# Last stage of a decoder block: row additions and splits on DVE, norm weights folded into the gate weights, finish of tiles after all additions

## Chip, cores and metric

The kernel runs on one core of a Trainium2 chip. The metric is the device time of one execution in microseconds; lower is better. Times of the kernel before are the median of three executions. One further execution was profiled, and every row below is from it.

## What is computed

One layer of a decoder over 512 tokens of 1024 float32 values. After attention and a mixture of experts it ends in a gated embedding and a norm; this end is the stage that the change rewrites:

```
h = h + moe_ffn(rmsnorm(h, g_ffn), ...)            # 8 expert rows per token, weighted, summed
h = h + (p @ w_ple) * sigmoid(rmsnorm(h, g_ple) @ w_ple_gate)
return rmsnorm(h, g_final)

def rmsnorm(x, g):
    r = rsqrt(mean(x * x, axis=-1) + 1e-6)
    return (x * r) * g
```

## The kernel before

The 512 tokens are four tiles (`NT`) of 128 partitions, the 1024 columns eight chunks (`KD`) of 128. Work is written by hand per engine; each engine runs its instructions in order and waits on semaphores (`E[...]` in the expert steps, `T[...]` in the last stage). The expert steps (`experts_*`) write each weighted expert row to `expert_rows` in HBM, 4096 rows of 1024 values (16 MB). The last stage (`tail_*`) does for each tile t:

- SP loads the tile's eight rows per token: tile 0 in four transfers of 1 MB ("quarters"), tiles 1 to 3 in two transfers of 2 MB each, n = 2 to 7, into four buffers of `ring`. Transfer n from 4 on waits for `took` to reach n - 3.
- `add_rows(t)`: the eight rows are added up and onto `h`. For tile 0 DVE does all (L1841, L1843). For tiles 1 to 3 DVE folds the first half (L1851, L1853) and adds it onto `h` (L1855), POOL folds the second half (L1732, L1734), and DVE adds that onto `h` (L1858, waits for `added`). Each addition onto `h` raises `took`.
- `turn_tile(t)` on PE transposes the tile, eight 128x128 blocks (L1759), after `took`.
- ACT takes them from PSUM, times `g_ple`, rounded to the format of the fast float32 product (`halves`, eight of 128x128, L1799); DVE computes what the rounding left off (`rests`, eight of 128x128, L1865).
- `gate_half(t, i)`: with each operand as a rounded part and a rest, PE needs three products per chunk, so 24 matmuls for each of the two column halves (L1774). `turn_tile(t + 1)` stands between the two halves.
- `squares`: ACT sums the squares of `h` (L1804), POOL makes the root (`root`, L1723 and L1725), ACT takes the sigmoid (L1812), `gated` on DVE multiplies by the embedding and adds onto `h` (L1873, L1875), then squares and a root again, and `finish` scales (L1880). SP stores the tile.

The gate weights `w_ple_gate` are split in the same way: ACT rounds (`wg_hi`, L1583), POOL computes the rest (`wg_lo`, L1720). DVE's order in `tail_vector` is written out; in the middle of it stand `gated(0)`, `rests(2)`, `finish(0)`, `add_rows(3)`, `gated(1)`, `rests(3)`, `finish(1)`.

Of the kernel before, what the change touches and what calls it, by code (L numbers as in the profile page):

```python
# [108 lines left out]
def build(nc, a, dbg=None):  # L109
# [8 lines left out]
    with ctx:  # L118
# [1434 lines left out]
        def experts_scalar(act):
# [9 lines left out]

            rows_in(0)
            for s in range(NS):
# [220 lines left out]
        def tail_scalar(act):
# [4 lines left out]
            act.wait_ge(s_gpk, 16)  # L1791

            def halves(t):
                if t >= 2:
                    act.wait_ge(T["mm"], 8 + 2 * (t - 1))
                for half in range(2):
                    act.wait_ge(T["turned"], 1 + 2 * t + half + 1)
                    for k in range(4 * half, 4 * half + 4):
                        last = nc.scalar.activation(x3[t % 2][:, 0, k, :], bank[BX3[t % 2][half]][:, (k % 4) * P:(k % 4 + 1) * P], ACT.Copy, scale=gpk[:, k:k + 1])  # L1799
                    last.then_inc(T["x_hi"], 1)  # L1800

            def squares(t, name, o):
                act.drain()
                nc.scalar.activation(junk, h[:, t, :], ACT.Square, scale=D ** -0.5, accum_out=part[:, o + t:o + t + 1]).then_inc(T[name], 1)  # L1804

            def sigmoids(t):
                act.wait_ge(T["rr"], t + 1)
                for i in range(2):
                    act.wait_ge(T["mm"], 8 + 2 * t + i + 1)
                    if t:  # L1810
                        act.wait_ge(T["gated"], 2 * (t - 1) + i + 1)
                    nc.scalar.activation(sigt[:, i * 512:(i + 1) * 512], bank[BG[t % 2][i]][:, :], ACT.Sigmoid, scale=part[:, 4 + t:5 + t]).then_inc(T["sig"], 1)  # L1812

            def last_squares(t):
                act.wait_ge(T["h3"], t + 1)
                squares(t, "ss2", 8)
# [141 lines left out]
```

## Time and profile before

| | us |
|---|---|
| median of 3 executions (lowest, highest) | 1277.23 (1275.13, 1278.48) |
| the profiled execution, its own time | 1278.9 |
| its span, first to last instruction | 1277.1 |
| busy in the span: PE, DVE, ACT, POOL | 1135.0, 472.5, 276.7, 320.2 |
| last expert matmul to the end of the span | 1156.7 to 1277.1 |

Times in rows are microseconds from the start of the span. A row of the timeline merges instructions that follow each other with the same line and operation (x gives how many) and names in brackets how long the engine had been idle before and what ended that. PE's clock has two levels, 1.2 and 2.4 GHz; "PEclk" is the granted share of the higher one.

### The profile page before, as it was taken

What the parts mean: (1) busy time and instruction counts of PE and PEld (TensorE: products, weight loads), DVE (VectorE), ACT (ScalarE), POOL (GpSimd) and SP (SyncE); (2) the same over time, 40 slices, a digit from 0 to 9 for tenths busy, and PEclk for the clock granted to TensorE, in tenths of its full rate; (3) what the DMA queues carried; (4) which work ended last, traced back from release to release, by engine and by line L of the source; (5) the groups of instructions that cost most, each with busy time, mean ns of one, the idle gap of its engine ahead of it and who ended that gap; (6) DMA issues with size and microseconds to landing.
All of it is one profiled execution on the core that took longest, in us unless ns stands there. A gap on an engine that the chain in (4) does not pass through costs nothing.

```text
span 1277.1 us, 19026 instructions
## 1 busy us (share of the span) xinstructions
PE 1135.0 (89%) x7561; PEld 663.3 (52%) x7562; DVE 472.5 (37%) x1050; ACT 276.7 (22%) x641; POOL 320.2 (25%) x218
## 2 busy tenths in 40 slices
PE   5999999999989899779999988998898999896476
PEld 4888786776767797434543333333333333332365
DVE  5245654564465634652222111211112211114475
ACT  3123333333345200101111111111111111114122
POOL 5522533333233210001111111111111111117360
PEclk9999999999989899779999988988999999998687
DMA  9821312222115124407999999999999999997611
GB/s 285 222 55 34 84 47 70 50 59 58 34 34 173 52 83 184 195 17 298 412 357 388 422 422 423 417 416 409 417 407 406 420 411 404 413 361 297 253 52 50
DMA packets 118424, 306.20 MB, mean 240 GB/s; under 512 B 21792, under 2 KB 80320, under 8 KB 92352
## 3 DMA queue, kind: packets, MB, share of 16 engines
q1 hardware_dynamic: 106096, 270.88, 55.6%
q0 software_dynamic: 12240, 34.09, 6.7%
q8 instruction: 61, 1.00, 0.3%
q14 instruction: 27, 0.22, 0.0%
HBM read 289.21 MB, written 26.21 MB: 247 GB/s over the span
## 4 chain that ended last, share of the span: by engine, by line
PE 25%; DMA 17%; issue 5%; POOL 3%; POOLq 2%; SPq 1%; DVE 0%; ACT 0%; ACTq 0%
DMA sb_gate_up<-in_w_up 17%; PE bank L1408 15%; PE bank L1432 7%; PE bank L1398 2%; POOL sb_w_gate_lo L1720 2%; POOLq L1733 1%; POOL sb_rows L1734 1%; SPq L963 1%; SPq L1443 0%; POOLq L1724 0%; PE bank L1415 0%; SPq L967 0%; POOL sb_small L1725 0%; PE bank L920 0%; DVE sb_xgT L1529 0%
## 5 line engine op out<-in xcount | busy, mean ns | idle before, releaser
L1408 PE MATMUL bank<-sb_gate_up,sb_xgT 128*32 128x512 f32 (+2 forms) x2144 | 312.6, 625 | 42.4 <-DMA sb_gate_up<-in_w_up 41.5
L1408 PEld LDWEIGHTS bank<-sb_gate_up,sb_xgT 128*32 128x32 f32 (+2 forms) x2144 | 98.3, 121 | 225.4 <-issue 221.4
L457 PE MATMUL bank<-sb_x_hl,sb_w_hl 128*128 128x512 f32 x768 | 200.4, 405 | 0.0
L1474 POOL DMA_INDIRECT expert_rows<-sb_rows_out,sb_work x42 | 42.2, 1004 | 474.4 <-DVE sb_rows_out L1535 474.4
L457 PEld LDWEIGHTS bank<-sb_x_hl,sb_w_hl 128*128 128x128 f32 x768 | 138.0, 189 | 43.5 <-issue 16.0
L1432 PE MATMUL bank<-sb_down,sb_work 128*32 128x512 f32 (+2 forms) x1072 | 153.3, 595 | 1.6 <-ACT sb_work L1573 0.6
L241 POOL TENSOR_TENSOR sb_w_hl<-sb_r,sb_w_hl 128x1024 fp32r<-128x1024 f32 x54 | 131.9, 2446 | 64.0 <-ACT sb_w_hl L1149 52.1
L1543 DVE TENSOR_TENSOR sb_work<-sb_work,bank 128x256 f32<-128x256 f32 x42 | 17.8, 423 | 333.2 <-ACT sb_work L1567 333.2
L235 POOL CAST sb_w_hl<-sb_r 128x1024 fp32r<-128x1024 f32 x35 | 37.6, 1075 | 205.6 <-PE bank L457 158.2
L1567 ACT ACTIVATE sb_work<-bank 128x256 f32<-128x256 f32 x42 | 16.2, 386 | 330.6 <-PE bank L1408 330.6
L1432 PEld LDWEIGHTS bank<-sb_down,sb_work 128*32 128x32 f32 (+2 forms) x1072 | 47.6, 116 | 73.3 <-issue 69.2
L770 ACT ACTIVATE sb_h<-sb_h,sb_small 128x128 f32<-128x128 f32 (+3 forms) x96 | 53.3, 556 | 133.3 <-DVE sb_small L665 133.2
L665 DVE CUSTOM_DVE_ANT_0 sb_h<-bank,sb_bias 128x128 f32<-128x128 f32 (+3 forms) x96 | 43.3, 488 | 103.7 <-PE bank L490 102.7
L1535 DVE TENSOR_SCALAR sb_rows_out<-bank,sb_work 128x512 f32<-128x512 f32 x42 | 31.5, 751 | 126.2 <-PE bank L1432 126.2
L956 POOL DMA_INDIRECT sb_xg<-xn_rows,sb_work x42 | 43.0, 1025 | 101.5 <-PE bank L1398 45.0
L1562 ACT ACTIVATE sb_rows_out<-bank,sb_work 128x512 f32<-128x512 f32 x42 | 28.9, 687 | 154.6 <-PE bank L1432 154.6
L1398 PEld LDWEIGHTS bank<-sb_cst,sb_xg 128*128 128x128 f32 x336 | 41.0, 192 | 34.5 <-issue 34.5
L1034 PE MATMUL bank<-sb_w_hl,sb_x_hl 128*128 128x256 f32 x384 | 48.6, 290 | 5.6 <-DVE sb_x_hl L1198 5.6
L1034 PEld LDWEIGHTS bank<-sb_w_hl,sb_x_hl 128*128 128x128 f32 x384 | 48.1, 199 | 6.0 <-issue 6.0
L1398 PE MATMUL bank<-sb_cst,sb_xg 128*128 128x128 f32 x336 | 47.8, 285 | 1.6 <-PEq L969 1.6
L780 ACT COPY sb_work<-bank 128x128 f32<-128x128 f32 (+4 forms) x104 | 40.3, 437 | 37.7 <-PE bank L503 32.5
L1022 PE MATMUL bank<-sb_x_hl,sb_w_hl 128*128 128x512 f32 x192 | 45.4, 399 | 2.9 <-PEq L372 2.9
(254 smaller groups left out, 1326.9 us busy)
## 6 DMA issues: line engine op xcount, KB each, us to landing
sb_gate_up<-in_w_gate SPq DMA_DIRECT2D x64, 1024.0 KB, 18.3
sb_gate_up<-in_w_up SPq DMA_DIRECT2D x64, 1024.0 KB, 24.3
sb_down<-in_w_down SPq DMA_DIRECT2D x64, 1024.0 KB, 18.2
sb_r<-in_w_in SPq DMA_DIRECT2D x34, 512.0 KB, 3.9
sb_rows<-expert_rows SPq DMA_DIRECT2D x6, 2048.0 KB, 9.3
sb_r<-in_w_out SPq DMA_DIRECT2D x8, 512.0 KB, 3.8
sb_rows<-expert_rows SPq DMA_DIRECT2D x4, 1024.0 KB, 7.8
sb_h<-in_x SPq DMA_DIRECT2D x4, 512.0 KB, 8.1
```

The costliest lines, as they stand in the source:

```text
L241: nc.gpsimd.tensor_tensor(w6_hl[:, slot, 1], raw_at[buf], w6_hl[:, slot, 0].bitcast(F32), ALU.subtract).then_inc(s_split, 1)
L457: last = nc.tensor.matmul(out[:, :], w6_hl[:, slot_at[n], zw, k, :], x_hl[:, zx, k, :], start=k + i == 0, stop=k == KD - 1 and i == 2)
L665: nc.vector.tensor_tensor_reduce(out=sc[:, i % 3, hh, 0:n_of(u)], in0=bank[BS[hh]][:, 0:n_of(u)], in1=bias[:, u["pair"] % 2, hh, S - n_of( ...
L770: nc.scalar.activation(sc[:, i % 3, hh, 0:n_of(u)], sc[:, i % 3, hh, 0:n_of(u)], ACT.Exp, scale=-1.0, bias=minus_max[:, i % 4, hh:hh + 1], ...
L780: nc.scalar.copy(pT[rows, i % 2, hh, 0:n], bank[BT[hh]][rows, 0:n]).then_inc(F["copied"], 1)
L956: nc.gpsimd.indirect_dma_start(out=xg[s % 2], out_offset=None, in_=xn2_d, in_offset=bass.IndirectOffsetOnAxis(ap=idx[:, s:s + 1], axis=0), ...
L1022: last = nc.tensor.matmul(bank[2 * (m % 4) + i][:, :], w6_hl[:, SLOT_OF[m], zw, k, :], x_hl[:, zx, k, :], start=k % 4 + j == 0, stop=k % 4 ...
L1034: last = nc.tensor.matmul(bank[t][:, (q % 2) * 256:(q % 2 + 1) * 256], x_hl[:, zx, k, t * P:(t + 1) * P], w6_hl[:, lo:lo + 2, zw, k, :], s ...
L1398: last = nc.tensor.transpose(bank[BX[half]][:, (k % 4) * P:(k % 4 + 1) * P], rows[:, k, :], ident)
L1408: last = nc.tensor.matmul(bank[BH][rows, :], xgT[:, k, rows], gate_up[slot_of[r]][:, :, k, :], start=k == 0, stop=k == KD - 1)
L1432: last = nc.tensor.matmul(bank[BO[i]][rows, :], hT[:, c, rows], Wd[slot_of[r]][:, c, i * 512:(i + 1) * 512], start=c == 0, stop=c == 1)
L1474: nc.gpsimd.indirect_dma_start(out=rows_d, out_offset=bass.IndirectOffsetOnAxis(ap=dst[:, s:s + 1], axis=0), in_=osb[s % 2], in_offset=Non ...
```

## The change

It moves no work before the last two expert steps. In the last stage:

1. POOL keeps only the roots. The folding of the second half of tiles 1 to 3 goes to DVE, in the same form as the first. The rests of the gate weights go to DVE too (`rest_of_gate`): two ahead of the last `rows_out` of the expert steps, six ahead of `add_rows(0)`.
2. `g_ple` is folded into the gate weights: `wg_hi` is the rounded product of weight and `g_ple`, `wg_lo` the rest of that product. The transposed tile is then only copied and subtracted, two instructions of 128x512 each on ACT and DVE in place of eight of 128x128. ACT rounds weight chunks 6 and 7 ahead of the copies of the turned `p` and of its last `rows_out`; the other six stay behind.
3. DVE's order is: additions and rests of all four tiles, then `gated(0)`, `gated(1)`, `finish(0)`, `gated(2)`, `finish(1)`, `finish(2)`, `gated(3)`, `finish(3)`. There are two buffers for the sigmoid.
4. Squares are summed by column halves, POOL adds the two sums (one more instruction per root); the second squares start on the first half. The sigmoid's table is loaded after the embeddings.
5. `turn_tile(t + 1)` stands after the first four chunks of `gate_part(t, 1)`.
6. SP issues `gfin` after the gate weights instead of before them.

```diff
@@ experts_sync @@
-            sp.dma_start(gfin, a["g_final"].partition_broadcast(P)).then_inc(s_gp, 16)
             w_gate_ple = chunks(a["w_ple_gate"][0])
...
                 sp.dma_start(wg_in[g][:, :, :], w_gate_ple[:, k:k + n]).then_inc(s_wg[g], 16)
+            sp.dma_start(gfin, a["g_final"].partition_broadcast(P)).then_inc(s_gp, 16)
@@ before rows_out(NS - 1) of experts_vector (n = 0, 1) and at the start of tail_vector (n = 2 to 7) @@
+        def rest_of_gate(n):
+            k = WG_ORDER[n]
+            nc.vector.wait_ge(T["w_hi"], n + 1)
+            nc.vector.scalar_tensor_tensor(out=wg_lo[k], in0=wg_raw[k], scalar=gpk[:, k:k + 1], in1=wg_hi[k].bitcast(F32),
+                                           op0=ALU.mult, op1=ALU.subtract).then_inc(T["w_lo"], 1)
@@ experts_scalar @@
+            for k in (6, 7):
+                round_gate(k)
             act.wait_ge(T["turned"], 1)
             for c in range(2):
                 nc.scalar.copy(pTt[:, c, :], bank[BX[c]][:, :]).then_inc(T["turned_sb"], 1)
             rows_out(NS - 1)
...
-                nc.scalar.copy(wg_hi[k], wg_raw[k]).then_inc(T["w_hi"], 1)
+            for k in range(6):
+                round_gate(k)
@@ tail_gpsimd @@
-                nc.gpsimd.tensor_tensor(wg_lo[k], wg_raw[k], wg_hi[k].bitcast(F32), ALU.subtract).then_inc(T["w_lo"], 1)
...
+                nc.gpsimd.tensor_tensor(part[:, o + t:o + t + 1], half_sums[:, o + 2 * t:o + 2 * t + 1], half_sums[:, o + 2 * t + 1:o + 2 * t + 2], ALU.add)
+                pool.drain()
...
-                nc.gpsimd.tensor_tensor(r[:, 0:2, :], r[:, 0:2, :], r[:, 2:4, :], ALU.add)
-                pool.drain()
-                nc.gpsimd.tensor_tensor(r[:, 0, :], r[:, 0, :], r[:, 1, :], ALU.add).then_inc(T["added"], 1)
@@ tail_tensor @@
             turn_tile(0)
             for t in range(NT):
-                gate_half(t, 0)
+                pe.wait_ge(T["x_lo"], 2 * t + 2)
+                gate_part(t, 0, range(KD))
+                gate_part(t, 1, range(4))
                 if t + 1 < NT:
                     turn_tile(t + 1)
-                gate_half(t, 1)
+                gate_part(t, 1, range(4, KD))
@@ tail_scalar @@
-                        last = nc.scalar.activation(x3[t % 2][:, 0, k, :], bank[BX3[t % 2][half]][:, (k % 4) * P:(k % 4 + 1) * P], ACT.Copy, scale=gpk[:, k:k + 1])
+                    nc.scalar.copy(x3[t % 2][:, 0, 4 * half:4 * half + 4, :], psv(BX3[t % 2][half], 4, P)).then_inc(T["x_hi"], 1)
...
             sigmoids(2)
-            last_squares(2)
-            sigmoids(3)
-            last_squares(3)
+            squares(0, "ss2", 8)
+            squares(1, "ss2", 8)
+            sigmoids(3, (0,))
+            squares(2, "ss2", 8)
+            sigmoids(3, (1,))
+            squares(3, "ss2", 8)
@@ tail_vector @@
-                dve.wait_ge(T["added"], t)
-                nc.vector.tensor_tensor(h[:, t, :], h[:, t, :], ring[(n + 1) % 4][:, 0, :], ALU.add).then_inc(T["took"], 1)
+                for n in (2 * t, 2 * t + 1):
+                    r = ring[n % 4]
+                    dve.wait_ge(s_rows[n % 4], 16 if n < 6 else 32)
+                    nc.vector.tensor_tensor(r[:, 0:2, :], r[:, 0:2, :], r[:, 2:4, :], ALU.add)
+                    dve.drain()
+                    nc.vector.tensor_tensor(r[:, 0, :], r[:, 0, :], r[:, 1, :], ALU.add)
+                    dve.drain()
+                    nc.vector.tensor_tensor(h[:, t, :], h[:, t, :], r[:, 0, :], ALU.add).then_inc(T["took"], 1)
+                    dve.drain()
...
+                    nc.vector.tensor_tensor(x3[t % 2][:, 1, ks, :], psv(BX3[t % 2][half], 4, P), x3[t % 2][:, 0, ks, :].bitcast(F32), ALU.subtract).then_inc(T["x_lo"], 1)
...
+            for t in range(NT):
+                add_rows(t)
+                rests(t)
             gated(0)
+            gated(1)
             finish(0)
+            gated(2)
             finish(1)
             finish(2)
             gated(3)
             finish(3)
```

The order of instructions on DVE before, from the last addition of tile 2 to the start of tile 3's additions (`sb_rows_*` are the buffers of `ring`, t_added is POOL's folding, t_rr2 the second root):

```order
L1858 TENSOR_TENSOR sb_h<-sb_h,sb_rows_5515 128x1024 [waits t_added]
L1873 TENSOR_TENSOR sb_emb<-sb_emb,sb_sig_ple 128x512 [waits t_sig]
L1875 TENSOR_TENSOR sb_h<-sb_h,sb_emb 128x512
L1873 TENSOR_TENSOR sb_emb<-sb_emb,sb_sig_ple 128x512 [waits t_sig]
L1875 TENSOR_TENSOR sb_h<-sb_h,sb_emb 128x512
L1865 SCALAR_TENSOR_TENSOR sb_x_0_5490<-bank,sb_g_ple,sb_x_0_5490 128x128 [waits t_x_hi]
L1865 SCALAR_TENSOR_TENSOR sb_x_0_5490<-bank,sb_g_ple,sb_x_0_5490 128x128 x3
L1865 SCALAR_TENSOR_TENSOR sb_x_0_5490<-bank,sb_g_ple,sb_x_0_5490 128x128 [waits t_x_hi]
L1865 SCALAR_TENSOR_TENSOR sb_x_0_5490<-bank,sb_g_ple,sb_x_0_5490 128x128 x3
L1880 SCALAR_TENSOR_TENSOR sb_h<-sb_h,sb_small,sb_ple_early 128x1024 [waits t_rr2]
L1851 TENSOR_TENSOR sb_rows_5516<-sb_rows_5516 128x2048 [waits t_rows2]
```

The same place in the changed kernel:

```order
L1856 TENSOR_TENSOR sb_rows_5516<-sb_rows_5516 128x2048 [waits t_rows1]
L1858 TENSOR_TENSOR sb_rows_5516<-sb_rows_5516 128x1024
L1860 TENSOR_TENSOR sb_h<-sb_h,sb_rows_5516 128x1024
L1867 TENSOR_TENSOR sb_x_0_5490<-bank,sb_x_0_5490 128x512 [waits t_x_hi] x2
L1856 TENSOR_TENSOR sb_rows_5517<-sb_rows_5517 128x2048 [waits t_rows2]
L1858 TENSOR_TENSOR sb_rows_5517<-sb_rows_5517 128x1024
L1860 TENSOR_TENSOR sb_h<-sb_h,sb_rows_5517 128x1024
```

The wait for POOL and the gated and finished tile are gone from between the additions; the second half's folding has come in.

ACT before, from the last step's hidden copy to the first rounding of a gate weight (t_turned is the turned `p`, s_wg2 the transfer of weight chunks 6 and 7):

```order
L1573 COPY sb_work<-bank 128x256 [waits e_hT_pe]
L1576 COPY sb_squares<-bank 128x512 [waits t_turned]
L1576 COPY sb_squares<-bank 128x512
L1562 ACTIVATE sb_rows_out<-bank,sb_work 128x512 [waits s_stored1,e_dn]
L1583 CAST sb_w_gate_hi_5512<-sb_w_gate_ple_5497 128x1024 [waits s_wg2,e_gu]
L1583 CAST sb_w_gate_hi_5513<-sb_w_gate_ple_5497 128x1024 [waits s_wg2]
```

And in the changed kernel:

```order
L1588 COPY sb_work<-bank 128x256 [waits e_hT_pe]
L1577 ACTIVATE sb_w_gate_hi_5513<-sb_w_gate_ple_5498,sb_g_ple 128x1024 [waits s_wg2,e_gu,s_gpk]
L1577 ACTIVATE sb_w_gate_hi_5514<-sb_w_gate_ple_5498,sb_g_ple 128x1024 [waits s_wg2]
L1595 COPY sb_squares<-bank 128x512 [waits t_turned]
L1595 COPY sb_squares<-bank 128x512
L1573 ACTIVATE sb_rows_out<-bank,sb_work 128x512 [waits s_stored1,e_dn]
```

Two roundings, with their wait for a transfer, now stand ahead of the last expert rows that ACT writes.

## Rows read from the trace of the kernel before

**Rows 1.** The view of waits, 1180 to 1278 us: total, times, longest

```profile
PE bank L1759 <- DVE sb_h L1858: 20.5, 3, 10.4
DVE sb_h L1858 <- POOL sb_rows L1734: 18.9, 2, 11.9
```

**Rows 2.** Timeline of PE: start, duration, instruction

```profile
1186.90 1.97 PE L1759 MATMUL bank<-sb_cst,sb_h 128*128 128x128 f32 x8 [15.32 <-DVE sb_h L1843]
1191.56 0.76 PE L1774 MATMUL bank<-sb_w_gate_hi,sb_x 128*128 128x512 f32 x1 [2.68 <-issue]
...
1195.10 0.65 PE L1774 MATMUL bank<-sb_w_gate_hi,sb_x 128*128 128x512 f32 x2
...
1198.63 0.40 PE L1774 MATMUL bank<-sb_w_gate_hi,sb_x 128*128 128x512 f32 x1
...
1247.93 1.97 PE L1759 MATMUL bank<-sb_cst,sb_h 128*128 128x128 f32 x8 [6.03 <-DVE sb_h L1858]
...
1267.82 0.39 PE L1774 MATMUL bank<-sb_w_gate_hi,sb_x 128*128 128x512 f32 x1
```

**Rows 3.** Timeline of DVE

```profile
1167.06 2.77 DVE L1841 TENSOR_TENSOR sb_rows<-sb_rows 128x1024 f32<-128x1024 f32 x1 [9.54 <-DMA sb_rows<-expert_rows]
1169.89 3.21 DVE L1843 TENSOR_TENSOR sb_h<-sb_h,sb_rows 128x1024 f32<-128x1024 f32 x1
...
1189.29 2.16 DVE L1865 SCALAR_TENSOR_TENSOR sb_x<-bank,sb_g_ple,sb_x 128x128 fp32r<-128x128 f32 x8 [2.45 <-ACT sb_x L1799]
1191.37 2.28 DVE L1851 TENSOR_TENSOR sb_rows<-sb_rows 128x2048 f32<-128x2048 f32 x1
1193.72 1.23 DVE L1853 TENSOR_TENSOR sb_rows<-sb_rows 128x1024 f32<-128x1024 f32 x1
...
1217.51 1.23 DVE L1855 TENSOR_TENSOR sb_h<-sb_h,sb_rows 128x1024 f32<-128x1024 f32 x1
...
1233.91 5.64 DVE L1880 SCALAR_TENSOR_TENSOR sb_h<-sb_h,sb_small,sb_ple_early 128x1024 f32<-128x1024 f32 x1 [1.93 <-POOL sb_small L1725]
1239.48 4.48 DVE L1851 TENSOR_TENSOR sb_rows<-sb_rows 128x2048 f32<-128x2048 f32 x1
...
1269.74 0.69 DVE L1875 TENSOR_TENSOR sb_h<-sb_h,sb_emb 128x512 f32<-128x512 f32 x1
1272.73 1.28 DVE L1880 SCALAR_TENSOR_TENSOR sb_h<-sb_h,sb_small,sb_ple_early 128x1024 f32<-128x1024 f32 x1 [2.29 <-POOL sb_small L1725]
```

**Rows 4.** Timeline of POOL

```profile
1159.43 22.43 POOL L1720 TENSOR_TENSOR sb_w_gate_lo<-sb_w_gate_ple,sb_w_gate_hi 128x1024 fp32r<-128x1024 f32 x8 [0.17 <-ACT sb_w_gate_hi L1583]
1191.62 2.12 POOL L1723 TENSOR_SCALAR sb_small<-sb_small 128x1 f32<-128x1 f32 x1 [9.76 <-ACT sb_squares L1804]
1200.61 0.57 POOL L1725 TENSOR_TENSOR sb_small<-sb_small,sb_cst 128x1 f32<-128x1 f32 x1 [6.87 <-issue]
...
1216.37 1.50 POOL L1725 TENSOR_TENSOR sb_small<-sb_small,sb_cst 128x1 f32<-128x1 f32 x1 [0.15 <-issue]
...
1271.76 0.22 POOL L1723 TENSOR_SCALAR sb_small<-sb_small 128x1 f32<-128x1 f32 x1 [10.22 <-ACT sb_squares L1804]
```

**Rows 5.** Timeline of ACT

```profile
1152.88 1.09 ACT L1576 COPY sb_squares<-bank 128x512 f32<-128x512 f32 x2
1156.76 0.69 ACT L1562 ACTIVATE sb_rows_out<-bank,sb_work 128x512 f32<-128x512 f32 x1 [2.79 <-PE bank L1432]
1157.35 7.66 ACT L1583 CAST sb_w_gate_hi<-sb_w_gate_ple 128x1024 fp32r<-128x1024 f32 x8
...
1188.12 2.17 ACT L1799 ACTIVATE sb_x<-bank,sb_g_ple 128x128 fp32r<-128x128 f32 x8 [15.91 <-PE bank L1759]
```

**Rows 6.** Transfers: landing of the gate weights (issued from 1131.25), then of tile 0's quarters (issued 1162.3 to 1163.6)

```profile
DMA to landing us min/median/max: 16.9/18.2/19.9
DMA to landing us min/median/max: 4.7/7.8/10.7
```

**Rows 7.** Stretch 1165 to 1194 us: engines' busy time, PEclk, DMA share, GB/s

```profile
1165.00:1194.00 29.00, 11.00 (x30) 6.21 (x29) 23.51 (x18) 7.51 (x19) 18.98 (x7) 0.67 0.99 415
```

More of the change, by code:

```diff
@@ L1386, in build @@
         assert at_moe <= WORK - 4096
-        T = {n: sem("t_" + n) for n in "turned turned_sb w_hi w_lo mm emb took added x_hi x_lo ss rr sig gated h3 ss2 rr2 out".split()}
+        T = {n: sem("t_" + n) for n in "turned turned_sb w_hi w_lo mm emb took x_hi x_lo ss rr sig gated h3 ss2 rr2 out".split()}
         s_p, s_gp, s_out = sem("s_p"), sem("s_gp"), sem("s_out")
@@ L1550, in experts_vector @@
                     rows_out(s - 1)
+            for n in range(2):
+                rest_of_gate(n)
             rows_out(NS - 1)
@@ L1790, in tail_scalar @@
                     nc.scalar.copy(emb[:, t, i * 512:(i + 1) * 512], bank[BE[t][i]][:, :]).then_inc(T["emb"], 1)
-            act.wait_ge(s_gpk, 16)
+            nc.scalar.activation(half_sums[:, 15:16], half_sums[:, 14:15], ACT.Sigmoid)
             def halves(t):
@@ L1797, in halves, with sigmoids @@
                     act.wait_ge(T["turned"], 1 + 2 * t + half + 1)
-                    for k in range(4 * half, 4 * half + 4):
-                        last = nc.scalar.activation(x3[t % 2][:, 0, k, :], bank[BX3[t % 2][half]][:, (k % 4) * P:(k % 4 + 1) * P], ACT.Copy, scale=gpk[:, k:k + 1])
-                    last.then_inc(T["x_hi"], 1)
+                    nc.scalar.copy(x3[t % 2][:, 0, 4 * half:4 * half + 4, :], psv(BX3[t % 2][half], 4, P)).then_inc(T["x_hi"], 1)
             def squares(t, name, o):
-                act.drain()
-                nc.scalar.activation(junk, h[:, t, :], ACT.Square, scale=D ** -0.5, accum_out=part[:, o + t:o + t + 1]).then_inc(T[name], 1)
-            def sigmoids(t):
+                for half in range(2):
+                    if o:
+                        act.wait_ge(T["h3"], 2 * t + half + 1)
+                    act.drain()
+                    nc.scalar.activation(junk[:, 0:512], h[:, t, 512 * half:512 * half + 512], ACT.Square, scale=D ** -0.5,
+                                         accum_out=half_sums[:, o + 2 * t + half:o + 2 * t + half + 1]).then_inc(T[name], 1)
+            def sigmoids(t, halves_of=(0, 1)):
                 act.wait_ge(T["rr"], t + 1)
-                for i in range(2):
+                for i in halves_of:
                     act.wait_ge(T["mm"], 8 + 2 * t + i + 1)
[L1810 to L1816, printed above, removed]
+                    if t >= 2:
+                        act.wait_ge(T["gated"], 2 * (t - 2) + i + 1)
+                    nc.scalar.activation(sigt[t % 2][:, i * 512:(i + 1) * 512], bank[BG[t % 2][i]][:, :], ACT.Sigmoid, scale=part[:, 4 + t:5 + t]).then_inc(T["sig"], 1)
             halves(0)
@@ L1863, in rests @@
                     dve.wait_ge(T["x_hi"], 2 * t + half + 1)
-                    for k in range(4 * half, 4 * half + 4):
-                        last = nc.vector.scalar_tensor_tensor(out=x3[t % 2][:, 1, k, :], in0=bank[BX3[t % 2][half]][:, (k % 4) * P:(k % 4 + 1) * P],
-                                                              scalar=gpk[:, k:k + 1], in1=x3[t % 2][:, 0, k, :].bitcast(F32), op0=ALU.mult, op1=ALU.subtract)
-                    last.then_inc(T["x_lo"], 1)
+                    ks = slice(4 * half, 4 * half + 4)
+                    nc.vector.tensor_tensor(x3[t % 2][:, 1, ks, :], psv(BX3[t % 2][half], 4, P), x3[t % 2][:, 0, ks, :].bitcast(F32), ALU.subtract).then_inc(T["x_lo"], 1)
             def gated(t):
@@ L1881, in finish @@
                                                op0=ALU.mult, op1=ALU.mult).then_inc(T["out"], 1)
+            for n in range(2, KD):
+                rest_of_gate(n)
             dve.wait_ge(s_gp, 16)
-            add_rows(0)
-            rests(0)
-            add_rows(1)
-            rests(1)
-            add_rows(2)
+            for t in range(NT):
+                add_rows(t)
+                rests(t)
             gated(0)
-            rests(2)
+            gated(1)
             finish(0)
-            add_rows(3)
-            gated(1)
-            rests(3)
+            gated(2)
             finish(1)
-            gated(2)
             finish(2)
```

67 lines of the change are left out of this document (23 added, 44 removed).

## The prediction

> **What bounds the kernel now.** I read the last stage from its waits outward, since the change touches nothing before the last two expert steps. The waits [rows 1] name the loop: from tile 1 on PE waits 20.5 us for DVE's last addition onto `h`, and DVE waits 18.9 us for POOL's folding. PE's timeline [rows 2] gives the milestones: turn of tile 0 at 1186.90, turn of tile 3 at 1247.93, last matmul over at 1268.21, end of the span at 1277.1. The stage is a chain of additions, turn, split and products per tile, and PE is not its bound: 24 products take 7.5 us or less. DVE's timeline [rows 3] shows two kinds of the same addition. While POOL computes the rests of the gate weights (1159.43 to 1181.86 [rows 4]) an addition of 128x1024 takes 2.77 to 3.21 us; alone it takes 1.23, and the 128x2048 one 2.28. The same 2048-wide fold takes 4.48 under POOL's folding of tile 3, and a `finish` 5.64 instead of 1.28. Transfers are not the cause: the 2.28 at 1191.37 fell in a stretch whose DMA share was 0.99 [rows 7].
>
> **The change, part by part.** I lay the new stage out from 1157 on.
>
> *Gate weights.* ACT is done with the hidden copy at 1152.88, where its two copies of the turned `p` began, and writes its last expert rows at 1156.76 after an idle 2.79 [rows 5]. Two roundings at 7.66 / 8 = 0.96 each and two copies (1.09) take it to 1155.9: 0.9 us to spare. The wait for chunks 6 and 7 is already met: issued from 1131.25, landed after 16.9 to 18.2, so by 1149.5 [rows 6], and `gfin` now stands behind them on SP, not before. DVE gets two rests at 1.28 (price of the same form, `finish` alone [rows 3]), from 1154.0 to 1156.7, just before its last `rows_out`: 0. Were ACT or DVE late there, everything behind would be. The other six rests need 6 x 1.28 = 7.7 us, from about 1158 to 1166; tile 0's first quarter lands at 1167.0 [rows 3, 6]. So the 22.4 us of POOL become 10.3 us of DVE under cover: cost 0, and if the cover were gone at most 7.7.
>
> *Tile 0.* Eight additions with their drains at 1.30 are 10.4: 1167.1 to 1177.5. The fourth quarter lands at 1163.6 + 10.7 = 1174.3 [rows 6], in time. Before, the turn began at 1186.90: **-9.4**.
>
> *Turn and split.* Before, 4.66 from turn to first product (1186.90 to 1191.56). ACT's first piece came 1.22 after the turn [rows 5]. Now ACT needs 0.6 per half (0.55 to 0.69 for a 512-wide instruction) and DVE 0.69: first half at 2.5, and the second, whose transposes end at 1.97, at 1.97 + 0.24 + 0.6 + 0.69 = 3.5. At full clock the transposes halve: 2.9. Eight instructions in two is cheaper on both engines (2.16 against 1.4), half of which was hidden.
>
> *Additions of tiles 1 to 3 on DVE.* Each half tile is 2.35 + 1.30 + 1.30 = 4.95, a tile 9.9. With the split a tile costs DVE 9.9 + 2.9 = 12.8. Tile 0's split ends at 1181.0. Tile 1's additions then end at 1190.9. PE first computes from 1181.1: eight products at the slow pace (1191.56 to 1195.10, 0.44 each), 28 at the fast one (1195.10 to 1198.63 for 15, 0.235 each [rows 2]), 10.1 us in all, so turn 1 begins at 1191.3. Split to 1194.2, additions to 1204.1 (turn 2), split to 1207.0, additions to 1216.9 (turn 3), split to 1219.8. Turn 0 to turn 3 takes 39.4 instead of 61.0: **-21.6**. Do the rows arrive? 4 MB by 1174.3, then 2 MB each 5.05 us at 415 GB/s [rows 7]: n = 2 to 7 at 1179.4, 1184.4, 1189.5, 1194.5, 1199.6, 1204.6, against needs at 1181.0, 1186.0, 1194.2, 1199.1, 1207.0, 1212.0. Buffers come free early enough (n = 7 after tile 1's additions, 1190.9).
>
> The Trainium skill (SBUF — State Buffer, A bandwidth-pool intuition that's wrong) gives about 358 GB/s between HBM and a core. This trace moved 415 over 29 us. By the page's rule the sum would rise by about 1 us, through tile 0 and the second half of tile 1.
>
> *PE behind it.* Between turn and split PE has four chunks of the older tile (12 products, 2.8 us), so it no longer idles there and should keep its clock. Tile 2's 36 products ahead of turn 3 run from 1208.0 to 1216.4. After turn 3 and the 12 products PE is free at 1220.8, and tile 3's 48 take 11.2: 1232.0. From turn 3 to the last matmul 15.1 instead of 20.3: **-5.2**. DVE and PE are here within 1 us of each other.
>
> *End.* `gated` of a tile is four of 0.69 with drains, 2.9. From 1219.8 DVE has gated 0 and 1 (to 1225.6), finish 0 (1.3, its root is ready near 1226), gated 2 (to 1230.5), finish 1. Finish 2 waits for squares and root after gated 2, about 2.3 (as 1270.43 to 1272.73 before), and ends near 1234.6; behind it in the queue stand the halves of gated 3, 2.9, to 1237.5. The last product alone would have allowed 1232.0 + 0.7 (sigmoid) + 1.5 = 1234.2. So from the last matmul to the last addition onto `h` it is 5.5 instead of 2.2: **+3.3**. After it, half a square less and one POOL instruction of 0.22 and a drain more cancel: 6.7 as before.
>
> *Roots among additions.* Unknown: what three roots do to DVE's additions. Under POOL's root instruction at 1216.37 (1.50 long) DVE's addition at 1217.51 still took 1.23 [rows 3, 4]: 0. The other bound is POOL's own busy time, three roots of about 1.0: 3.0. The nearest row says 0, which I take. POOL is slowed (2.12 for 0.22 at 1191.62), and its first root had a gap of 6.87 us ahead of the power. Root 0 would then be ready by about 1195, and ACT's turn-2 work, the first thing queued behind its sigmoid, is due at 1204.9.
>
> The Trainium skill (SBUF — State Buffer, Who interferes with whom) says that a DVE instruction with two SBUF inputs and a GpSimd instruction that reads SBUF lock each other out for a whole instruction. That is what rows 3 show of the large folds; for the small ones they show no loss on DVE. By the page three roots cost up to 3 us, and the sum would be 1247.
>
> **Sum.** -9.4 - 21.6 - 5.2 + 3.3 = -32.9: the span 1277.1 becomes 1244.2, the profiled execution's 1278.9 becomes 1246.0. That execution stood 1.7 above the median, so against the median 1277.23 I get 1244.3; with a little for handoffs, **1245**.
>
> **Rivals.**
> 1. *The clock.* Tile 0's products start at half pace, and each fall costs about eight products at 0.44 instead of 0.235, 1.7 us. If PE's short gaps let it fall again at each tile, three times, 5 us: **1250**. For: tile 0's products before began slow, after 15.32 us of idling [rows 2]. Against: the gaps are now under 2 us and filled.
> 2. *Roots late.* If POOL gets its port only when DVE pauses, the first root with its 6.87 us gap is ready only at 1205. ACT then holds turn 2 behind two sigmoids, and each tile loses some 2 us, with DVE's stalls 3 more: **1252**. For: the 2.12. Against: POOL came through at the end of one DVE instruction each time.
> 3. *The last expert step slips.* ACT has 0.9 us of room and DVE about none; if the two rests take 3 us more there (POOL issues its scatter at that time), the rows leave later and all slides: **1248**.
> 4. *Slow additions stay* (slower). If the long additions came from the loads and not from POOL, DVE would pay for them on the path now: eight of tile 0 at 3.2 instead of 1.23 (+15.8) and six half tiles at 4.48 + 2 x 3.2 instead of 4.74 (+36.8), 52.6 in all: **1297**. It decides from 63% of that extra (32.9 of 52.6), about 1.25 us more per 128x1024 addition. Against: 2.28 and 1.23 beside a DMA share of 0.99.
> 5. *Finish 2 does not hold gated 3*, and PE sets the end: 3.3 less, **1241**.
>
> **How the numbers follow.** Forecast 64%, clock 10%, roots late 9%, expert step 6%, end set by PE 7%, slow additions 2%, something I don't see 2%. The median's own uncertainty is under 0.3%, about 3.8 us, which is what counts as no change. All cases but the fourth and a share of the unseen are faster by far more: faster 0.96, same 0.01, slower 0.03. The forecast's terms may be off by some 4 us together (the roots' 0 to 3, handoffs, 1 of landing), rivals 1 to 3 add up to 7, and the fifth takes 4: 1239 to 1255.
>
> **What would show it.** Right: no POOL wait in DVE's waits; additions of 1.23 and 2.28 from 1167 on; turns near 1177.5, 1191, 1204, 1217; last product near 1232; a DVE wait for the root of tile 2 with gated 3 behind it. Wrong: additions above 1.5 us (rival 4), slow PEclk after 1190 (1), a sigmoid that ACT holds for a root with turned blocks waiting (2), the last expert matmul's rows written after 1157.5 (3). A turn 3 later than 1222 would break the forecast.

## The result and the profile after

| us | before | changed |
|---|---|---|
| median | 1277.53 (4 runs) | 1244.12 (4 runs, 1243.09 to 1246.06) |
| span of the profiled execution | 1277.1 | 1241.2 |
| DVE's last expert rows start | 1156.76 | 1154.80 |
| from there to the end of the span | 120.3 | 86.4 |
| POOL busy in the span | 320.2 | 283.6 |

The ratio is 0.9743, 95% interval 0.9725 to 0.9761: 33 us or 2.6% faster, against the 1245 on record. The third and fourth lines of the table matter for all that follows. The expert steps end 2.0 us earlier in this execution. That is scatter between executions: a second profile of the changed kernel (C0 below) has DVE's last expert rows at 1156.64, as late as the kernel before. So I compare the **last stage**, from the start of DVE's last `rows_out` to the end of the span: 120.3 before, 86.4 now, 33.9 less. C0 gives 86.1, and E8, the kernel before with one load moved, gives 119.2, so differences of a few tenths of this measure say nothing, and one of 1 us needs rows that show where it arises.

The view of waits of the changed kernel, 1150 to 1242 us (total, times, longest), which answers to [rows 1]:

```profile
PE bank L1765 <- DVE sb_h L1848: 6.5, 1, 6.5
DVE sb_h L1879 <- POOL sb_small L1740: 4.2, 3, 2.2
DVE sb_rows L1846 <- DMA sb_rows<-expert_rows: 1.9, 1, 1.9
PE bank L1778 <- DVE sb_x L1867: 1.4, 1, 1.4
PE bank L1765 <- DVE sb_h L1860: 0.4, 2, 0.2
```

DVE waits for POOL 4.2 us, in the finishes alone. PE's 20.5 us behind the additions of tiles 1 to 3 have become 0.4.

PE's timeline, the turns and the last product, for [rows 2]:

```profile
1176.11 1.97 PE L1765 MATMUL bank<-sb_cst,sb_h 128*128 128x128 f32 x8 [6.49 <-DVE sb_h L1848]
1179.48 0.79 PE L1778 MATMUL bank<-sb_w_gate_hi,sb_x 128*128 128x512 f32 x1 [1.40 <-DVE sb_x L1867]
...
1190.31 1.03 PE L1765 MATMUL bank<-sb_cst,sb_h 128*128 128x128 f32 x8
...
1202.69 1.10 PE L1765 MATMUL bank<-sb_cst,sb_h 128*128 128x128 f32 x8 [0.18 <-DVE sb_h L1860]
...
1215.18 1.09 PE L1765 MATMUL bank<-sb_cst,sb_h 128*128 128x128 f32 x8 [0.24 <-DVE sb_h L1860]
...
1229.86 0.39 PE L1778 MATMUL bank<-sb_w_gate_hi,sb_x 128*128 128x512 f32 x1
```

Tile 0's turn still takes 1.97, the others 1.03 to 1.10. PE's clock is down for that turn and for about the first 12 products behind it (0.43 each until about 1184.5, 0.23 after), and up from there on. The idle times in brackets ahead of turns 2 and 3 are 0.18 and 0.24; turn 1 has none.

DVE's timeline, for [rows 3]: the rests of the gate weights, tile 0, tile 1, the start of tile 2, then the end from the last half of `gated(2)` (1227.58), with `finish` of tiles 1, 2 and 3.

```profile
1152.12 2.48 DVE L1400 SCALAR_TENSOR_TENSOR sb_w_gate_lo<-sb_w_gate_ple,sb_g_ple,sb_w_gate_hi 128x1024 fp32r<-128x1024 f32 x2 [1.28 <-ACT sb_w_gate_hi L1577]
1154.80 0.75 DVE L1544 TENSOR_SCALAR sb_rows_out<-bank,sb_work 128x512 f32<-128x512 f32 x1 [0.20 <-PE bank L1441]
1156.56 7.26 DVE L1400 SCALAR_TENSOR_TENSOR sb_w_gate_lo<-sb_w_gate_ple,sb_g_ple,sb_w_gate_hi 128x1024 fp32r<-128x1024 f32 x6 [1.00 <-ACT sb_w_gate_hi L1577]
1165.71 1.22 DVE L1846 TENSOR_TENSOR sb_rows<-sb_rows 128x1024 f32<-128x1024 f32 x1 [1.89 <-DMA sb_rows<-expert_rows]
1167.01 1.23 DVE L1848 TENSOR_TENSOR sb_h<-sb_h,sb_rows 128x1024 f32<-128x1024 f32 x1
...
1179.35 2.28 DVE L1856 TENSOR_TENSOR sb_rows<-sb_rows 128x2048 f32<-128x2048 f32 x1
1181.70 1.23 DVE L1858 TENSOR_TENSOR sb_rows<-sb_rows 128x1024 f32<-128x1024 f32 x1
1183.00 1.23 DVE L1860 TENSOR_TENSOR sb_h<-sb_h,sb_rows 128x1024 f32<-128x1024 f32 x1
...
1192.77 2.28 DVE L1856 TENSOR_TENSOR sb_rows<-sb_rows 128x2048 f32<-128x2048 f32 x1
...
1227.58 0.69 DVE L1875 TENSOR_TENSOR sb_h<-sb_h,sb_emb 128x512 f32<-128x512 f32 x1
1228.19 1.28 DVE L1879 SCALAR_TENSOR_TENSOR sb_h<-sb_h,sb_small,sb_ple_early 128x1024 f32<-128x1024 f32 x1
1230.65 1.28 DVE L1879 SCALAR_TENSOR_TENSOR sb_h<-sb_h,sb_small,sb_ple_early 128x1024 f32<-128x1024 f32 x1 [1.18 <-POOL sb_small L1740]
...
1234.02 0.69 DVE L1875 TENSOR_TENSOR sb_h<-sb_h,sb_emb 128x512 f32<-128x512 f32 x1
1236.91 1.29 DVE L1879 SCALAR_TENSOR_TENSOR sb_h<-sb_h,sb_small,sb_ple_early 128x1024 f32<-128x1024 f32 x1 [2.20 <-POOL sb_small L1740]
```

Every addition, those not printed here too, is at its undisturbed 1.22 to 1.23 or 2.28 to 2.29. DVE had 0.20 us to spare ahead of its last `rows_out`, and 1.89 ahead of the first quarter.

POOL's timeline, for [rows 4]: root 0, then the first instruction of root 1 and of the last root.

```profile
1180.41 1.27 POOL L1736 TENSOR_TENSOR sb_small<-sb_small 128x1 f32<-128x1 f32 x1 [23.11 <-ACT sb_squares L1811]
1188.64 0.66 POOL L1738 TENSOR_SCALAR sb_small<-sb_small 128x1 f32<-128x1 f32 x1 [6.96 <-issue]
1189.46 0.57 POOL L1740 TENSOR_TENSOR sb_small<-sb_small,sb_cst 128x1 f32<-128x1 f32 x1 [0.16 <-issue]
1193.70 1.40 POOL L1736 TENSOR_TENSOR sb_small<-sb_small 128x1 f32<-128x1 f32 x1 [3.67 <-ACT sb_squares L1811]
...
1235.59 0.19 POOL L1736 TENSOR_TENSOR sb_small<-sb_small 128x1 f32<-128x1 f32 x1 [4.98 <-ACT sb_squares L1811]
```

The same instruction takes 1.40 beside DVE's additions and 0.19 when DVE is idle. The gap of 6.96 is there again, one instruction into the first root.

The stretch table (busy times, PEclk, DMA share, GB/s), for [rows 7]:

```profile
1165.00:1190.00 25.00, 17.11 (x54) 11.69 (x53) 20.58 (x16) 5.96 (x12) 2.47 (x3) 0.80 1.01 430
1190.00:1230.00 40.00, 39.58 (x183) 31.64 (x181) 32.90 (x32) 16.36 (x37) 15.08 (x18) 1.00 0.31 133
```

From 1190 to 1230 PE is busy 39.6 of 40 us at the full clock.

### The profile page after: what moved, and what is told of

It is laid out like the page before. It is cut to its first block, busy times and chain, and to the rows that moved or that the text cites. A ratio compares the mean times of both kernels' runs of the same rounds, so it can differ in the third digit from the quotient of the medians.

```text
span 1241.2 us, 19016 instructions
## 1 busy us (share of the span) xinstructions
PE 1128.7 (91%) x7561; PEld 657.8 (53%) x7562; DVE 473.6 (38%) x1040; ACT 275.9 (22%) x634; POOL 283.6 (23%) x212
## 4 chain that ended last, share of the span: by engine, by line
PE 27%; DMA 17%; issue 5%; SPq 2%; POOLq 1%; POOL 1%; DVE 0%; ACT 0%
DMA sb_gate_up<-in_w_up 17%; PE bank L1417 16%; PE bank L1441 8%; PE bank L1407 2%; SPq L963 1%; POOLq L1737 1%; POOL sb_small L1740 1%; SPq L1452 1%; PE bank L1424 0%; SPq L967 0%; POOLq L1739 0%; PE bank L920 0%; DVE sb_xgT L1538 0%; DVE sb_h L1879 0%; PE bank L1527 0%
## 5 line engine op out<-in xcount | busy, mean ns | idle before, releaser
L1407 PEld LDWEIGHTS bank<-sb_cst,sb_xg 128*128 128x128 f32 x336 | 41.0, 192 | 34.5 <-issue 34.5
L1407 PE MATMUL bank<-sb_cst,sb_xg 128*128 128x128 f32 x336 | 47.9, 285 | 1.6 <-PEq L969 1.6
```

What stands on the lines that cost most here:

```text
L1407: last = nc.tensor.transpose(bank[BX[half]][:, (k % 4) * P:(k % 4 + 1) * P], rows[:, k, :], ident)
```

## Experiments

Three theories could explain 33 us: POOL's large instructions slow DVE and hand over late (mine), the order on DVE alone does it, or the small split instructions and PE's order do. Each of E1 to E5 undoes one part of the changed kernel; no run undoes two of these parts together. All medians are given with their ratio to the kernel before on the same chip; the last stage of the one profiled execution of each (86.4 in the changed kernel) is the finer measure, free of the expert steps.

**E1, gate weights' rests on POOL.** ACT rounds the bare weight, and POOL subtracts it as before. `g_ple` is then applied nowhere, so this kernel leaves a factor out of the result; it serves for timing alone. DVE computes none of the eight rests.

```diff
-            for n in range(2):
-                rest_of_gate(n)
...
-                nc.scalar.activation(wg_hi[k], wg_raw[k], ACT.Copy, scale=gpk[:, k:k + 1]).then_inc(T["w_hi"], 1)
+                nc.scalar.copy(wg_hi[k], wg_raw[k]).then_inc(T["w_hi"], 1)
...
+            for n, k in enumerate(WG_ORDER):
+                pool.wait_ge(T["w_hi"], n + 1)
+                nc.gpsimd.tensor_tensor(wg_lo[k], wg_raw[k], wg_hi[k].bitcast(F32), ALU.subtract).then_inc(T["w_lo"], 1)
...
-            for n in range(2, KD):
-                rest_of_gate(n)
```

> The changed kernel, but POOL computes the eight rests of the gate weights again (22 us from about 1157). g_ple is left out of the computation here (ACT rounds the bare weight, so POOL can subtract as before). If POOL's large instructions are what slowed DVE's additions of tile 0: these take about 3.0 instead of 1.23 again, turn 0 comes 8 to 9 us later than in the changed kernel, and all behind it slides: 1252 to 1254 us. Rival, the loads or the late start of the stage slowed them: additions stay at 1.23, about 1244 us. Between: DVE wins most of its conflicts and the cost is 3 to 5 us.

Measured: 1252.93, ratio 0.9803 (0.9782 to 0.9823); last stage 95.2, so 8.8 more, and turn 0 is 8.8 later too. DVE's timeline of E1, tile 0:

```profile
1165.98 2.50 DVE L1847 TENSOR_TENSOR sb_rows<-sb_rows 128x1024 f32<-128x1024 f32 x1 [9.78 <-DMA sb_rows<-expert_rows]
1168.57 3.21 DVE L1849 TENSOR_TENSOR sb_h<-sb_h,sb_rows 128x1024 f32<-128x1024 f32 x1
...
1178.80 2.82 DVE L1847 TENSOR_TENSOR sb_rows<-sb_rows 128x1024 f32<-128x1024 f32 x1 [0.46 <-issue]
1181.69 1.23 DVE L1849 TENSOR_TENSOR sb_h<-sb_h,sb_rows 128x1024 f32<-128x1024 f32 x1
```

The same loads, the same addresses, another neighbour: up to 3.21 until POOL is done at 1180.5, then 1.23. This part is worth 8.8 us.

**E2, second half folded on POOL**, as in the kernel before, with everything else changed.

```diff
@@ tail_gpsimd @@
-            for t in range(NT):
+            root(0, 0, "")
+            for t in range(1, NT):
...
+                nc.gpsimd.tensor_tensor(r[:, 0:2, :], r[:, 0:2, :], r[:, 2:4, :], ALU.add)
+                pool.drain()
+                nc.gpsimd.tensor_tensor(r[:, 0, :], r[:, 0, :], r[:, 1, :], ALU.add).then_inc(T["added"], 1)
                 root(t, 0, "")
...
@@ tail_vector @@
+                    if n % 2:
+                        dve.wait_ge(T["added"], t)
+                        nc.vector.tensor_tensor(h[:, t, :], h[:, t, :], r[:, 0, :], ALU.add).then_inc(T["took"], 1)
+                        dve.drain()
+                        continue
```

> The changed kernel, but POOL folds the second half of tiles 1 to 3 again, between its first roots, and DVE only adds the result onto h. If the handover to POOL is a loss: root 0 with its gap of 7 us stands ahead of tile 1's folding, so turn 1 comes about 8 us later, and each further tile some 2 us more: 1254 to 1258 us. Rival, sharing helps once the weights and finishes are out of the way: DVE saves 3.7 us per tile, PE becomes the bound, 1240 to 1243 us.

Measured: 1261.32, ratio 0.9875 (0.9853 to 0.9897); last stage 103.5, 17.1 more, beyond what I expected. POOL's and DVE's timelines of E2, tile 2:

```profile
1202.44 1.29 POOL L1736 TENSOR_TENSOR sb_small<-sb_small 128x1 f32<-128x1 f32 x1 [5.59 <-ACT sb_squares L1818]
1203.89 1.17 POOL L1738 TENSOR_SCALAR sb_small<-sb_small 128x1 f32<-128x1 f32 x1 [0.16 <-issue]
1205.21 1.51 POOL L1740 TENSOR_TENSOR sb_small<-sb_small,sb_cst 128x1 f32<-128x1 f32 x1
1206.69 4.61 POOL L1747 TENSOR_TENSOR sb_rows<-sb_rows 128x2048 f32<-128x2048 f32 x1
1211.44 2.35 POOL L1749 TENSOR_TENSOR sb_rows<-sb_rows 128x1024 f32<-128x1024 f32 x1
```

```profile
1213.82 1.23 DVE L1864 TENSOR_TENSOR sb_h<-sb_h,sb_rows 128x1024 f32<-128x1024 f32 x1 [7.54 <-POOL sb_rows L1749]
```

Turn 1 comes 21.8 us after turn 0 instead of 14.2 (I had said 8 us more, it is 7.6; most of it is an idle stretch of 6.96 inside POOL's root 0), and behind it a tile's period is 16.9 us instead of 12.4 to 12.5. The folding does not run beside the tile but stands behind the previous tile's root, which waits for that tile's squares and whose three instructions take 4.3 us beside DVE's additions. No engine waits for the rows there. I had priced 2 us per further tile; it is 4.4 to 4.6. Of that 0.7 comes from PE, whose turns are back at 1.97. DVE's additions stay at 1.22 to 1.23: POOL folds while DVE waits, so this loss is all handover and none of it slower additions.

The price is that of the queue order of the kernel before. What POOL's folding costs if it stands ahead of the previous root, and so runs beside DVE's folding, no run here tests.

**E3, finish between the additions**: the old order on all three engines.

```diff
@@ tail_vector @@
-            for t in range(NT):
-                add_rows(t)
-                rests(t)
...
+            add_rows(2)
             gated(0)
+            rests(2)
+            finish(0)
+            add_rows(3)
             gated(1)
-            finish(0)
+            rests(3)
+            finish(1)
             gated(2)
-            finish(1)
```

> The changed kernel with the old order on DVE, ACT and POOL: gated 0 ahead of tile 2's split, finish 0 ahead of tile 3's additions, gated 1 ahead of tile 3's split. If order alone matters: turn 3 comes 6 us later (2.9 of gated, 3.2 of finish with its wait), the last product about 9 later, and the end gives back the 2 us that finish 2 costs now: 1250 to 1253 us. Rival, DVE's sum of work is the bound and the order is indifferent: 1244 us.

Measured: 1249.99, ratio 0.9781 (0.9762 to 0.9801); last stage 90.8, 4.4 more. Turn 3 began 17.58 after turn 2 (1202.76 to 1220.34) instead of 12.49, and at half clock again. The last product came 6.6 us later, not the 9 I had expected, and the end gave 2.2 of it back. DVE's timeline of E3 names the larger part of the price, a `finish` with its wait ahead of tile 3's additions; the other part is `gated(0)`, 2.8 us (1202.80 to 1205.58):

```profile
1209.21 1.29 DVE L1881 SCALAR_TENSOR_TENSOR sb_h<-sb_h,sb_small,sb_ple_early 128x1024 f32<-128x1024 f32 x1 [2.35 <-POOL sb_small L1740]
```

Order matters, but for about an eighth of the gain.

**E4, `g_ple` on the tile again**, eight instructions of 128x128.

> The changed kernel, but g_ple multiplies the transposed tile again: eight instructions of 128x128 per tile on ACT and on DVE instead of two of 128x512 each. Turn to first product at full clock about 3.4 instead of 2.5 us, four times on the path: +3.5 to +4.5, 1248 us. Rival, the small pieces pipeline behind the transposes and cost nothing: 1244 to 1245 us.

```diff
-                    nc.scalar.copy(x3[t % 2][:, 0, 4 * half:4 * half + 4, :], psv(BX3[t % 2][half], 4, P)).then_inc(T["x_hi"], 1)
+                    for k in range(4 * half, 4 * half + 4):
+                        last = nc.scalar.activation(x3[t % 2][:, 0, k, :], bank[BX3[t % 2][half]][:, (k % 4) * P:(k % 4 + 1) * P], ACT.Copy, scale=gpk[:, k:k + 1])
+                    last.then_inc(T["x_hi"], 1)
...
```

DVE's subtraction goes back to eight pieces in the same way, and the gate weights are rounded and subtracted without `g_ple`.

Measured: 1250.61, ratio 0.9785 (0.9767 to 0.9803); last stage 92.0, 5.6 more, one beyond the range. ACT's timelines of tile 1, first E4, then the changed kernel:

```profile
1193.01 2.17 ACT L1804 ACTIVATE sb_x<-bank,sb_g_ple 128x128 fp32r<-128x128 f32 x8 [10.72 <-PE bank L1764]
```

```profile
1190.94 1.08 ACT L1804 CAST sb_x<-bank 128x512 fp32r<-128x512 f32 x2 [10.62 <-PE bank L1765]
```

ACT's part doubles. At full clock one of its pieces takes 0.27 us and a transpose 0.13, so little hides. From the start of the turn to the end of the split it is 3.9 to 4.0 us instead of 2.5 to 2.6 for tiles 1 to 3, and 4.4 instead of 3.2 for tile 0.

**E5, turn between the halves**: 24 products instead of 12 behind the turn.

```diff
-                gate_part(t, 1, range(4))
                 if t + 1 < NT:
                     turn_tile(t + 1)
-                gate_part(t, 1, range(4, KD))
+                gate_part(t, 1, range(KD))
```

> The changed kernel with turn t+1 between the two halves of the gate products again, finish 2 still ahead of gated 3. The last product comes 2.8 us later, but gated 3 waits for finish 2 anyway, some 2.2 us: only 0.6 to 0.9 us longer than the changed kernel. Rival, PE's position is worth its full 2.8 us.

Measured: 1246.38, ratio 0.974 (0.9715 to 0.9766); last stage 88.0, 1.6 more, where I had expected 0.6 to 0.9. The ratios cannot tell this from the changed kernel; the profile can. The last product came 3.0 us later, counted from the last expert rows, of which 1.4 was hidden. What I had missed: tile 2's sigmoid comes late too, and ACT has it ahead of the first second square, so `finish(0)` waited 2.23 for its root instead of 0.83.

The next four ran on one chip. **C0** is the changed kernel, **E6** swaps two calls on DVE, **E6b** is E6 with E5's order on PE, **E7** is E6 with a shorter last root.

```diff
             gated(2)
             finish(1)
+            gated(3)
             finish(2)
-            gated(3)
             finish(3)
```

> The changed kernel itself, as the measure for the other three on the same chip: ratio to the kernel before about 0.974.

> The changed kernel with gated 3 ahead of finish 2 on DVE. If finish 2, waiting for its root, holds gated 3: the last addition onto h comes at sigmoid + 1.5 instead of 4.4 us after the last product, so 2.2 us less: ratio to the changed kernel 0.9982. Rival, PE's last product or ACT sets the end: no difference.

> As the one with gated 3 ahead of finish 2, but turn t+1 stands between the two halves of the gate products again, so 24 products in place of 12 lie behind it on PE. If PE's position matters: the last product comes 12 x 0.233 = 2.8 us later, and with nothing on DVE to hide it the time is 2.8 us above that variant, 0.6 above the changed kernel. Rival, DVE's additions are the only bound: equal to that variant.

> As the one with gated 3 ahead of finish 2, and the last root shortened: DVE adds both half sums and the epsilon in one instruction, POOL only takes the power (0.8 us of POOL against some 0.2 of DVE, -0.5), and finish 3 and its store go by column halves (-0.6). Expected 3.3 us below the changed kernel, ratio 0.9973. Rival, each further handoff costs what it saves: as that variant, 2.2 below.

| | median | ratio (interval) | last stage |
|---|---|---|---|
| C0 | 1244.49 | 0.9719 (0.9700 to 0.9738) | 86.1 |
| E6 | 1241.54 | 0.9703 (0.9683 to 0.9723) | 84.5 |
| E6b | 1243.88 | 0.9717 (0.9694 to 0.9740) | 86.5 |
| E7 | 1240.00 | 0.9690 (0.9671 to 0.9708) | 83.7 |

The intervals overlap, so the ratios alone do not separate these four. The medians and the last stage agree that E7 is lowest and E6 next; for C0 and E6b they disagree. By the last stage E6 gains 1.6 where 2.2 was expected. DVE's timeline of E6 has `gated` of the last half directly behind its sigmoid and `finish(2)` behind that.

```profile
1235.62 0.69 DVE L1873 TENSOR_TENSOR sb_emb<-sb_emb,sb_sig_ple 128x512 f32<-128x512 f32 x1 [0.19 <-ACT sb_sig_ple L1820]
1236.40 0.69 DVE L1875 TENSOR_TENSOR sb_h<-sb_h,sb_emb 128x512 f32<-128x512 f32 x1
1237.01 1.28 DVE L1879 SCALAR_TENSOR_TENSOR sb_h<-sb_h,sb_small,sb_ple_early 128x1024 f32<-128x1024 f32 x1
1239.47 1.28 DVE L1879 SCALAR_TENSOR_TENSOR sb_h<-sb_h,sb_small,sb_ple_early 128x1024 f32<-128x1024 f32 x1 [1.18 <-POOL sb_small L1740]
```

E6b is 2.0 longer than E6 and so loses more than E6 gained. Its last product comes 2.0 later than that of E6, and nothing on DVE covers that any more. I had expected 2.8; its turn 3 was 0.8 earlier. E7 is another 0.8 below E6, where 1.1 was expected. In it DVE adds the half sums and epsilon (0.15), POOL only takes the power, and the last tile is finished and stored by halves:

```diff
...
+            nc.vector.scalar_tensor_tensor(out=part[:, 11:12], in0=half_sums[:, 14:15], scalar=EPS, in1=half_sums[:, 15:16],
+                                           op0=ALU.add, op1=ALU.add).then_inc(T["last"], 1)
+            dve.wait_ge(T["rr2"], 4)
+            for i in range(2):
...
```

By its median it is the fastest version that ran, about 3.1% below the kernel before.

**E8, the kernel before with only the load of `g_final` moved.** This tests whether the 2.0 us in the expert steps belong to the change.

> The kernel before, with only the load of g_final moved behind the gate weights on SP. The changed kernel's profile has its last expert rows 2.0 us earlier than that of the kernel before. If the earlier gate weights did that: ratio 0.9985, last rows written at 1154.8. If it is the scatter of the expert steps between executions: ratio 1.000.

Measured: ratio 0.9999 (0.9984 to 1.0014). Its profile has the last expert rows at 1153.49, and the other profiles of the changed kernel and its variants have them at 1154.5 to 1160.4. The changed kernel alone has 1154.80 in one profile and 1156.64 in the other (C0). So this place scatters by about 2 us. The move shows no effect, though the interval would just allow the 0.15% that was the other case.

**E9 and E10, POOL work beside the additions.** The changed kernel, with work on POOL that shares no written data with DVE. Each ran in a single execution, so only the rows of its profile are used.

```diff
+            scratch = sb("pool_scratch", N0, [P, 384])[:, :]
+            pool.wait_ge(s_gp, 16)
+            pool.wait_ge(s_quarter[0], 16)
+            for _ in range(12):
+                nc.gpsimd.tensor_tensor(scratch, gfin[:, 0:384], gfin[:, 384:768], ALU.add)
+                pool.drain()
```

E10 has `nc.gpsimd.memset(scratch, 0.0)`, 24 times, in its place.

> The changed kernel, and POOL adds two pieces of g_final (128x384) into an unused place twelve times while DVE adds up tile 0. If POOL's reads block DVE's second input: each addition of tile 0 takes 1.23 plus up to one POOL instruction, some 2 us, until POOL is done. Rival, DVE was slowed only by what it shared data with: 1.23.

> As the one with twelve additions on POOL, but POOL only writes: 24 fills of 128x384. If only reads collide, the additions stay at 1.23; if any large POOL instruction collides, they grow as with the reads.

POOL's gap of 6.8 us put most of the work beside tile 1 rather than tile 0. Timelines of POOL and DVE, E9:

```profile
1175.08 1.60 POOL L1746 TENSOR_TENSOR sb_pool_scratch<-sb_ple_early 128x384 f32<-128x384 f32 x1 [6.86 <-issue]
1176.83 20.09 POOL L1746 TENSOR_TENSOR sb_pool_scratch<-sb_ple_early 128x384 f32<-128x384 f32 x10 [0.15 <-issue]
```

```profile
1182.98 2.28 DVE L1862 TENSOR_TENSOR sb_rows<-sb_rows 128x2048 f32<-128x2048 f32 x1
1185.34 1.87 DVE L1864 TENSOR_TENSOR sb_rows<-sb_rows 128x1024 f32<-128x1024 f32 x1
1187.28 1.87 DVE L1866 TENSOR_TENSOR sb_h<-sb_h,sb_rows 128x1024 f32<-128x1024 f32 x1
```

And E10:

```profile
1178.01 12.23 POOL L1746 MEMSET sb_pool_scratch<- 128x384 f32 x23 [6.83 <-issue]
```

```profile
1187.17 1.23 DVE L1864 TENSOR_TENSOR sb_rows<-sb_rows 128x1024 f32<-128x1024 f32 x1
1188.47 1.23 DVE L1866 TENSOR_TENSOR sb_h<-sb_h,sb_rows 128x1024 f32<-128x1024 f32 x1
```

POOL instructions that read cost 0.64 to 0.66 us on five of tile 1's six additions; the first, at 1182.98, kept its 2.28. POOL's own take 2.0 on average there, while the first of the twelve, which began ahead of DVE's addition, took 0.99. Instructions that only write cost nothing. Last stage: 90.3 with reads, 85.8 with writes. So the collision needs no data that the two engines share.

## Why the prediction was right

Counted from DVE's last expert rows, predicted and measured: turn 0 at 20.7 and 21.3, turn 1 at 34.5 and 35.5, turn 2 at 47.3 and 47.9, turn 3 at 60.1 and 60.4, the last product's end at 75.2 and 75.4, the last addition onto `h` over at 80.7 and 79.9, the end of the span at 87.4 and 86.4. The sum came out at -33.9 instead of -32.9, with three of its four terms off by 0.4 to 1.2 us, partly against each other. By the terms of the sum:

- *Gate weights, cost 0.* Right, as E1 shows from the other side: 8.8 us if left on POOL. On DVE the eight rests took 1.21 to 1.24 each and ended before the first quarter. ACT's roundings were 1.05 us apart rather than 0.96, which left 0.7 us on ACT and 0.20 on DVE ahead of the last expert rows, where I had counted 0.9 and none.
- *Tile 0, -9.4.* Measured -8.8. The additions ran as priced; the first quarter landed 0.6 us later after the expert rows than before.
- *Turns 0 to 3, -21.6.* Measured 39.1 instead of 39.4 us: -22.0. For tiles 1 and 2 the split took 2.5 us (1190.31 to 1192.77 for tile 1) instead of my 2.9. That 2.9 was a slip: my own terms, with the transposes at 0.99, give 0.99 + 0.24 + 0.6 + 0.69 = 2.5. Against that, 12 and not 8 products of tile 0 ran at the slow pace. Turn 1 waits for PE by my layout too, by 0.4 us; it waited 1.1 (additions over at 1189.22, turn at 1190.31). That the total came within 0.4 is in part the luck of these two.
- *Last tile on PE, -5.2.* Measured 15.1 from turn 3 to the last product's end, as predicted.
- *End, +3.3.* Measured +2.1 (10.95 us against 8.89). The mechanism is the one named, `finish(2)` holding `gated(3)`, and E6 confirms it by 1.6 us. `finish(2)` could start 2.4 us after `gated(2)` was over (1228.27 to 1230.65), as priced. The size was off elsewhere. From turn 3 to the end of `gated(2)` it took 13.1 us and not 13.6, 0.3 of it the split again. The 1234.6 for the end of `finish(2)` was a slip, since 1230.5 + 2.3 + 1.3 = 1234.1, and the last `gated` and what follows it took 0.3 less.
- *Roots among additions, 0.* Right: DVE shows 1.22 to 1.23 and 2.28 to 2.29 under every root, while POOL's instructions grew to as much as 1.50. The Trainium skill (SBUF — State Buffer, Who interferes with whom) puts the collision on POOL instructions that read SBUF, and says that the later one is blocked. E9 and E10 agree with the first half: reads cost DVE 0.64 to 0.66, writes nothing. For POOL's 128x1 instructions no run here shows a loss on DVE, so the up to 3 us that I had worked out from that section did not occur.
- *Landing.* 430 GB/s from 1165 to 1190, above the 415 I used. The Trainium skill (SBUF — State Buffer, A bandwidth-pool intuition that's wrong) has 358 for this path, and this trace moved more. No wait for rows occurred after the first quarter.

The rivals: slow additions (4) are excluded by the rows and by E10; roots late (2) did not occur, since root 0 was ready at 1190.0, 3.5 us before ACT came to its sigmoid at 1193.5 and 13 us before the split of tile 2 behind it (1203.4); the clock (1) was down at tile 0 alone; the expert step (3) held with 0.2 us to spare; the fifth is what E6 makes of the kernel.

The losses of E1 to E5 are 8.8, 17.1, 4.4, 5.6 and 1.6, 37.5 together against 33.9. The parts seem to overlap little, which fits that all lie on one chain of additions, turn, split and products, but it is not shown, since no run undoes two of them. By far the largest is taking POOL's folding, as it was queued, out of that chain.

## What to carry to other kernels

Work given to a second engine helps only if it truly runs beside the first. Before splitting a fold between DVE and POOL, look whether DVE's instructions with two inputs from SBUF grow while POOL reads, and what stands ahead of POOL's share in its queue; here 3.7 us more of DVE work per tile replaced 7 us of POOL work plus its wait behind a root. Whether a share that POOL can start early would do better was not tried. On an engine that works in order, put the instruction whose input is late behind those whose input is ready, and check it again at the very end, where nothing covers it.

## What the runs showed of the hardware

- A two-input addition on DVE (128x1024, 1.23 us alone) takes 3.2 beside POOL subtractions of 128x1024 (kernel before, E1), 1.87 beside POOL additions of 128x384 (E9), and 1.23 beside POOL fills of 128x384 (E10) and beside POOL's 128x1 instructions (changed kernel), which grow themselves from 0.19 to 1.40 and from 0.57 to 1.50.
- In all 14 profiles POOL is idle in the last stage once for 6.8 to 7.0 us, put down to issue, between its first instruction there that a drain follows and the next: ahead of the power before, ahead of the epsilon in the changed kernel, after one addition in E9 and after one fill in E10. The eight subtractions of the gate weights, which no drain follows, ran without it in the kernel before and in E1. What it is was not tested; no wait of another engine hung on it except in E2 and in the kernel before, where tile 1's folding stood behind it.
